# Ropes moved inside a branch, indexer heads in pairs, samples' values in two passes, a final tile in halves: one change to a two-layer hybrid encoder

## The reference, cut to what matters

```
# mixer A: rotary on queries, keys and indexer; 4 indexer heads score all keys
a_q = rope(heads(a_q), pos);  i_q = rope(i_q.reshape(B, T, N_IDX, IDX_DIM), pos)
dots  = einsum('bqhd,bkd->bqhk', qi, ki) * IDX_DIM ** -0.5
score = einsum('bqhk,bqh->bqk', relu(dots), wi)
top_val, top_idx = top_k(where(adm, score, NEG), topk)      # then softmax over the chosen keys
# mixers B and C: v = xn @ w_v for 8 heads of 64, and attention over all admissible keys
branch = einsum('btnw,nwd->btnd', o, w_branch)
x = x + einsum('btnd,btnd->btd', sigmoid(xn @ w_gate), branch) @ w_out
x = x + (silu(g) * u) @ w_down                              # g, u: convolved rows of rmsnorm(x) @ w_up
y = rmsnorm(x, norm_final)
```

## Time and profile before

| | |
|---|---|
| median of 3 executions | 2195.29 us (2191.95 to 2202.59) |
| profiled execution, its own time | 2195.33 us |
| its span | 2193.5 us |
| TensorE (PE) busy | 2148.7 us, 98% |
| VectorE (DVE) busy | 1342.6 us, 61% |
| ScalarE (ACT) busy | 955.0 us, 44% |
| mean granted TensorE clock | 0.995 of full speed |

### The profile page before, as it was taken

The page is one execution under the profiler, slowest core; times in us unless marked ns, Lnnn a source line. Parts: engine busy times, 40 slices in busy tenths (PEclk is TensorE's granted clock), DMA queues, the critical chain, the costliest instruction groups (busy, mean ns, idle before and its releaser), DMA issues.

```text
span 2193.5 us, 40057 instructions
## 1 busy us (share of the span) xinstructions
PE 2148.7 (98%) x16226; PEld 2023.5 (92%) x16226; DVE 1342.6 (61%) x2486; ACT 955.0 (44%) x1543; POOL 196.0 (9%) x144
## 2 busy tenths in 40 slices
PE   7999999999999999999999999999999999999997
PEld 7798999897899999999998889888979999999997
DVE  6558636765566773576365686377656477636753
ACT  3346414634634662344332572156255266524432
POOL 0000000000022110011310100000000311100122
PEclk9999999999999999999999999999999999999998
DMA  5231133121122223222232212221211222232223
GB/s 193 59 108 40 58 97 111 40 78 39 49 78 77 86 86 87 87 85 87 96 104 68 92 39 87 84 95 49 71 40 55 84 80 80 88 91 86 86 87 103
DMA packets 51795, 176.10 MB, mean 80 GB/s; under 512 B 6032, under 2 KB 8672, under 8 KB 51664
## 3 DMA queue, kind: packets, MB, share of 16 engines
q1 hardware_dynamic: 44496, 158.81, 23.4%
q0 software_dynamic: 2848, 10.54, 1.2%
q10 hardware_dynamic: 4320, 4.87, 0.7%
HBM read 161.30 MB, written 12.90 MB: 79 GB/s over the span
## 4 chain that ended last, share of the span: by engine, by line
PE 96%; DVE 3%; ACT 1%; DMA 0%; issue 0%; SPq 0%; DVEq 0%; ACTq 0%
PE d L1230 61%; PE d L1273 14%; PE ab L1306 4%; PE ab L1527 2%; PE d L1570 2%; PE d L1579 2%; PE d L1306 1%; PE d L1444 1%; PE ab L1352 1%; PE ab L1230 1%; PE ab L1557 1%; PE ab L1519 1%; PE ab L1520 1%; DVE ol L813 1%; PE ab L1257 0%; PE d L1398 0%
## 5 line engine op out<-in xcount | busy, mean ns | idle before, releaser
L410 ACT ACTIVATE wh<-raw 128x512 fp32r<-128x512 f32 x580 | 365.7, 631 | 839.6 <-PE d L1230 697.0
L710 DVE TENSOR_TENSOR wl<-raw,wh 128x512 fp32r<-128x512 f32 x580 | 402.8, 696 | 410.0 <-ACT wh L410 400.6
L1230 PE MATMUL d<-xh,wh 128*128 128x288 f32 x2400 | 513.9, 295 | 17.7 <-DMA cf<-in_const 14.5
L1230 PE MATMUL d<-xl,wh 128*128 128x288 f32 x2400 | 510.4, 293 | 0.0
L1230 PE MATMUL d<-xh,wl 128*128 128x288 f32 x2400 | 510.4, 293 | 0.0
L1230 PEld LDWEIGHTS d<-xh,wh 128*128 128x128 f32 x2400 | 383.1, 188 | 21.2 <-DMA cf<-in_const 14.5
L1230 PEld LDWEIGHTS d<-xh,wl 128*128 128x128 f32 x2400 | 382.6, 188 | 0.0
L1230 PEld LDWEIGHTS d<-xl,wh 128*128 128x128 f32 x2400 | 382.4, 188 | 0.0
L1273 PE MATMUL d<-xh,wh 128*128 128x288 f32 x768 | 174.8, 309 | 0.0
L1273 PE MATMUL d<-xh,wl 128*128 128x288 f32 x768 | 164.9, 296 | 0.0
L1273 PE MATMUL d<-xl,wh 128*128 128x288 f32 x768 | 164.8, 296 | 0.0
(11 more groups left out here) (309 smaller groups left out, 3197.9 us busy)
## 6 DMA issues: line engine op xcount, KB each, us to landing
raw<-in_w SPq DMA_DIRECT2D x290, 512.0 KB, 3.5
out_o_k<-k POOLq DMA_DIRECT2D x4, 1152.0 KB, 7.2
out_o_v<-v POOLq DMA_DIRECT2D x4, 1024.0 KB, 8.7
x<-in_xT SPq DMA_DIRECT2D x8, 288.0 KB, 6.4
out_y<-z SPq DMA_DIRECT2D x8, 288.0 KB, 2.3
k<-in_bc_k_past ACTq DMA_DIRECT2D x4, 512.0 KB, 4.7
v<-in_bc_v_past ACTq DMA_DIRECT2D x4, 512.0 KB, 5.6
cf<-in_const SPq DMA_DIRECT2D x1, 896.0 KB, 8.1
```

The lines of the kernel that those rows point to most:

```text
L410: act.activation(wh[:, c % SPLIT_SLOTS, :], raw[v_ % 2][:, (c % 2) * 512:(c % 2) * 512 + 512], ACT.Copy).then_inc(high_done, 1)
L710: dve.tensor_tensor(wl[:, c % SPLIT_SLOTS, :], raw[(c // 2) % 2][:, (c % 2) * 512:(c % 2) * 512 + 512], wh[:, c % SPLIT_SLOTS, :].bitcast( ...
L1230: ins = pe.matmul(outs[half], w_, r_[:, kk, HALF * half:HALF * half + HALF], start=first and n == 0, stop=last and n == len(kks) - 1)
```

## The change

What it does, part by part:

1. **Start.** `cf` is loaded after the second raw unit, masks after the third; TensorE waits for `s_const` only before the first `norm_sum`, which now stands in the middle of the third projection. ACT and DVE split six chunks in the opening instead of four. The casts of the constants move behind the first takes on DVE (`constants()`).
2. **Indexer.** Heads 0 and 1, then 2 and 3, go together: one head in rows 0 to 63 of the array, the other in rows 64 to 127, in two banks. Steps stand between half projections (`project_half`). The sums of the forget gate on DVE move into the projection of values.
3. **Values.** For the samples `xp` holds the 64 high columns and the 64 low columns of x side by side (`pair_samples`, two DVE copies per branch). The fifth token tile then takes 2 passes, not 3; DVE adds the two row halves.
4. **B, p = 0.** Four gate blocks stand ahead of `logits_x`.
5. **A.** `turn_query(2)` and `turn_query(3)`, with their ropes, move into pairs 0 and 1, behind the second `turn`; `scores_next(0)` waits for the second rope only and stands between the halves of query projection 3. DVE and ACT order follows.
6. **Branch output.** `branch_first` does the high products of j = 0 and j = 1, then the low products of both.
7. **FFN norm.** The square of the last tile of x is made by ACT and added by DVE; Pool squares seven tiles.
8. **End.** The last tile is computed for tokens 0 to 287, then 288 to 575, each with its own norm and outputs; 16 stores. The two weight units beyond the end are not loaded any more.

The core of the diff:

```diff
@@ sync @@
+            sp.dma_start(raw[1][:], w[1]).then_inc(landed[1], 16)
             sp.dma_start(cf[:], const).then_inc(s_const, 16)
-            sp.dma_start(raw[1][:], w[1]).then_inc(landed[1], 16)
-            sp.dma_start(w1[:, 0:M_END], masks).then_inc(s_masks, 16)
...
@@ vector @@
                 low_parts(l, 9)
+                if l == 0:
+                    constants()
+                pair_samples()
                 wait_taken(dve, l, D_KI)
                 rope(l, 0, ki, norm_both)
...
+            def pair_samples():
+                dve.tensor_copy(xp[:, :, 0:TS], xh[:, :, TP:T].bitcast(F32))
+                dve.tensor_copy(xp[:, :, TS:2 * TS], xl[:, :, TP:T].bitcast(F32)).then_inc(samples_paired, 1)
...
                 for m in (B, C, A):
                     for j in range(2 if m == B else 0, 4):
+                        if m == B:
+                            index_adds(j - 2, 0)
+                            index_adds(j - 2, 1)
+                        if m == A and j == 3:
+                            scale_step(l, m, 0, 0)
                         low_parts(l, 2 * U_Q[m] + 2 * j + 4)
...
-                        if m == A and j:
+                        if m == A and j in (1, 2):
                             wait_taken(dve, l, D_Q[m] + j - 1)
                             rope(l, 2 + j, q[:, j - 1, :], perm_both)
...
                         gate_take(l, m, 2 * p)
+                        if m == A and p < 2:
+                            rope(l, 5 + p, q[:, 2 + p, :], perm_both)
                         max_step(l, m, p, 3)
...
+                dve.wait_ge(acc_ready, 2 * l + 2)
+                dve.wait_ge(last_square, l + 1)
+                dve.tensor_tensor(sumsq[:], sumsq[:], tmp[:], ALU.add).then_inc(last_sum, 1)
@@ gpsimd @@
-                for j in range(KD):
+                for j in range(KD - 1):
                     wait_taken(pool, l, D_OUT + j)
                     square(j)
@@ tensor @@
             def branch_first(l, m):
...
                 pe.wait_ge(dfree[d % 2], freed(l, d))
+                for j in range(2):
+                    pe.wait_ge(low_done, l * CHUNKS + c + j + 1)
+                    for kk in range(4):
+                        if j == 0:
+                            pe.wait_ge(oh_ready, l * 12 + 4 * m + kk + 1)
+                        products(j, kk, wh, oh, first=kk == 0)
+                        products(j, kk, wl, oh)
+                    if j == 0:
+                        pe.wait_ge(o_ready, l * 3 * PAIRS + PAIRS * m + PAIRS)
+                        pe.sem_inc(dfree[1 - gate_bank(m)], HEADS)
+                        pe.wait_ge(dfree[(d + 1) % 2], freed(l, d + 1))
+                for j in range(2):
+                    for kk in range(4):
+                        if j == 0:
+                            pe.wait_ge(ol_ready, l * 12 + 4 * m + kk + 1)
+                        ins = products(j, kk, wh, ol, last=kk == 3)
+                    ins.then_inc(chunks, 1)
...
+                for w_, f_, l_ in ((wh, True, False), (wl, False, True)):
+                    ins = pe.matmul(src(4), xp[:, kk, :], w_[:, c % SPLIT_SLOTS, cols:cols + n],
...
-            pe.wait_ge(s_const, 16)
...
+                def index_heads(pair, s):
+                    if pair or s > 1:
+                        pe.wait_ge(relus, l * 8 + 4 * pair + s - 1)
+                    if s < 3:
+                        t = I_QT[s]
+                        for i, r in enumerate(ROWS):
+                            ins = pe.matmul(ab[:, 2 * (s % 2) + i, 0:tile_keys(t)], iq[r, pair, t * P:(t + 1) * P], k2[r, 1, 0:tile_keys(t)], start=True, stop=True)
+                    else:
+                        for a, n, key in ((0, PAST, T), (PAST, TS, TP)):
+                            for r in ROWS:
+                                ins = pe.matmul(ab[r, 2, a:a + n], iq[r, pair, TP:T], k2[r, 1, key:key + n], start=True, stop=True)
...
+                        for pair in range(2):
+                            index_heads(pair, 0)
+                            index_heads(pair, 1)
+                            project_half(l, U_Q[B] + 2 + pair, D_Q[B] + 2 + pair, 0)
+                            index_heads(pair, 2)
+                            index_heads(pair, 3)
+                            project_half(l, U_Q[B] + 2 + pair, D_Q[B] + 2 + pair, 1)
...
-                            project(l, U_Q[A] + 3, D_Q[A] + 3)
-                            turn_query(2)
-                            gate_blocks(l, m, 0, range(0, 2))
-                            turn_query(3)
-                            gate_blocks(l, m, 0, range(2, 4))
-                            pe.wait_ge(roped, l * 8 + 8)
+                            project_half(l, U_Q[A] + 3, D_Q[A] + 3, 0)
+                            pe.wait_ge(roped, l * 8 + 6)
                             scores_next(0)
+                            project_half(l, U_Q[A] + 3, D_Q[A] + 3, 1)
+                            gate_blocks(l, m, 0, range(0, 4))
...
+                            if m == A and p < 2:
+                                turn_query(2 + p)
+                                gate_blocks(l, m, 2 * p + 1, range(0, 2))
+                                pe.wait_ge(roped, l * 8 + 7 + p)
+                                scores_samples(p)
+                                gate_blocks(l, m, 2 * p + 1, range(2, 4))
...
+            down_half(0, range(FH)).then_inc(first_half, 1)
+            down_half(1, range(0, 4))
+            pe.wait_ge(acc_ready, 1 + 2 * LAYERS)
+            sum_half(0, sumsq, stop=False)
+            pe.wait_ge(last_sum, LAYERS + 1)
+            sum_half(0, tmp, start=False).then_inc(norms, 1)
+            sum_half(1, sumsq, stop=False)
+            down_half(1, range(4, FH)).then_inc(chunks, 3)
+            pe.wait_ge(last_sum, LAYERS + 2)
+            sum_half(1, tmp, start=False).then_inc(norms, 1)
```

More of the change, by code:

```diff
@@ L680, in _ @@
                     round_a(f, FH - 1)
-                    for c in range(24):
+                    last = f and l == LAYERS - 1
+                    if last:
+                        act.preload_act_table_set("natural_log_exp_and_others")
+                    for c in range(24 - SPLIT_SLOTS if last else 24):
                         high_part(l * CHUNKS + f * (2 * U_HALF), l * (UNITS // 2) + f * (U_HALF // 2), 2 * U_DOWN + 4 + c)
@@ L1230, in dense @@
                             ins = pe.matmul(outs[half], w_, r_[:, kk, HALF * half:HALF * half + HALF],
-                                            start=first and n == 0, stop=last and n == len(kks) - 1)
+                                            start=first and n == 0 and begin, stop=last and n == len(kks) - 1 and end)
                     if n % 4 == 3 or n == len(kks) - 1:
@@ L1236, in no_wait, with sum_half @@
                 pass
+            def sum_half(half, squares, start=True, stop=True):
+                return pe.matmul(norm_out[half], cf[:, C_ONE:C_ONE + P], squares[:, HALF * half:HALF * half + HALF], start=start, stop=stop)
             def norm_sum(count):
-                pe.wait_ge(acc_ready, count)
-                for half in range(2):
-                    ins = pe.matmul(norm_out[half], cf[:, C_ONE:C_ONE + P], sumsq[:, HALF * half:HALF * half + HALF], start=True, stop=True)
-                ins.then_inc(norms, 1)
+                if count % 2:
+                    pe.wait_ge(acc_ready, count)
+                else:
+                    pe.wait_ge(last_sum, count // 2)
+                sum_half(0, sumsq)
+                sum_half(1, sumsq).then_inc(norms, 1)
             def xn_wait(l, r):
@@ L1290, in branch_first, with products @@
-                pe.wait_ge(o_ready, l * 3 * PAIRS + PAIRS * m + PAIRS)
-                pe.sem_inc(dfree[1 - gate_bank(m)], HEADS)
-                for kk in range(4):
-                    pe.wait_ge(ol_ready, l * 12 + 4 * m + kk + 1)
-                    for half in range(2):
-                        ins = pe.matmul(dhalf[d % 2][half], hi_w[:, kk * P:kk * P + P], ol[:, kk, HALF * half:HALF * half + HALF],
-                                        start=False, stop=kk == 3)
-                ins.then_inc(chunks, 1)
+                def products(j, kk, weights, heads, first=False, last=False):
+                    for half in range(2):
+                        ins = pe.matmul(dhalf[(d + j) % 2][half], weights[:, (c + j) % SPLIT_SLOTS, kk * P:kk * P + P],
+                                        heads[:, kk, HALF * half:HALF * half + HALF], start=first, stop=last)
+                    return ins
@@ L1304, in by_token @@
                     o = src(t)
                     for x_, w_, f_, l_ in ((xh, wh, True, False), (xh, wl, False, False), (xl, wh, False, True)):
-                        ins = pe.matmul(o, x_[:, kk, a:a + P], w_[:, c % SPLIT_SLOTS, cols:cols + n],
-                                        start=first and f_ and starts(t), stop=last and l_, skip_group_check=True)
```

(10 more changed lines are left out.)

350 lines of the change are left out of this document (205 added, 145 removed).

## The result

The changed kernel took 2180.28 us (four executions, 2179.25 to 2181.17), the kernel before 2195.36 us in the same comparison. The ratio is 0.993, 95% interval 0.990 to 0.995: faster, by 15 us and not by the 42 forecast, and outside the range of 2145 to 2165. The profiled execution has a span of 2177.4 us.

What follows compares the result with a forecast made beforehand. PE, busy 98% of the span, was taken as the bound, leaving only matmul time and its pauses or slow stretches. Eight terms, -5.0 -10.6 -7.4 -2.6 -12.0 +3.0 -3.0 -4.5 = -42.1, took 2195.3 to 2153 us; range 2145 to 2165.

Steps and rivals of the forecast that it cites:

- At the upper level a 288-column matmul costs 0.13 us: All TensorE work at the 2.4 GHz granted clock: one price per matmul, 6.4 us for a projection of 48.
- the first rival: Branch A: new waits eat more, each bringing some 3 us at 1.2 GHz; +12, 2165 us; 0.22 together with head-pair rival.
- a sign of being wrong: Anywhere in the kernel: a PE wait over 3 us or a mean clock under 0.99 would disprove the forecast.
- The spell at the lower level: Branch A, kernel before: some 3 us per layer lost to the lower clock after PE's waits.
- its list of signs: Whole kernel: expected trace marks, such as first matmul near 8.3 us and 10.4 us from last matmul to end.
- the second (no overlap of heads): Indexer: head pairs don't overlap; +9.6 us, 2163 us; chance 0.22 together with the first rival.
- the third (hidden waits): Rope waits (4.8 us) or bank waits (7.8 us) are hidden after all: 2148 or 2145, both 2140; chance 0.14.
- the fourth (a lower clock: TensorE throughout: fewer pauses lower the granted clock; 21.5 us per hundredth, about 2205 us at 0.97; chance 0.02.
- the fifth: Somewhere in the new order: an unseen wait keeps the change from doing what it says; 2170 to 2190 us; chance 0.05.

Runs made afterwards that it cites:

- e13: Changed kernel with the FFN's norm sum issued two matmuls later in both layers, no instruction added; 2159.21 us.
- e3: Changed kernel with the FFN norm change alone undone, so Pool squares the last x tile again; 2163.78 us.
- e15: Changed kernel with the FFN's norm sum issued four matmuls later in the first layer, six in the second; 2170.06 us.
- e11: Changed kernel with DVE making the constants and sample pairs later, in idle time; 2175.59 and 2176.19, 2166.34 and 2166.50 us.
- e5: Changed kernel with the branch output change alone undone, going tile by tile again; 2155.20 us.
- e4: Kernel before with the FFN norm change alone: ACT squares the last x tile, DVE adds it; 2191.03 us.
- e6: Changed kernel with extra 288-column matmuls right ahead of the FFN's norm sum, two in the first layer, four in the second; 2170.97 us.
- e1: Changed kernel with two extra 512-column matmuls right behind each layer's norm sum in the FFN; 2180.67 us.
- e2: Changed kernel with extra 512-column matmuls in varied numbers behind FFN norm sums, in branch outputs and ahead of second projections; 2176.69 us.
- e10: Changed kernel with A's output tile by tile, earlier B/C takes, later constants, plus 512-column probes in five branch outputs and an extra matmul before layer 1's norm sum; 2160.60 us.

## Why the prediction was wrong, step by step

The step that failed is not one of the eight parts: it is the sentence "At the upper level a 288-column matmul costs 0.13 us", used as if the more than 10,000 of them that the change leaves alone would keep their price: a term of zero, without a reason given. The runs showed +21.0 us in its place, at 133.3 instead of 130.0 ns a matmul. The rivals had a price for the clock, but the clock was 0.998; what changed was the rhythm at the same clock. Whether the rows of the kernel before could have shown it is another matter: its stretch behind branch A already ran at 133.3 ns (592 successive distances in layer 1), and I took one price for all. With the norm sum moved by two matmuls, the changed kernel takes 2159.2, inside the range; 6 us are then left against 2153, half of them in part 1. Another 1.7 or so is a spell that the first rival had in mind, only elsewhere: in the profile of e13, and in those of e3 and e15, the wait of 3.4 us for the small tile is followed by 3.4 us of matmuls 0.24 apart. The changed kernel's own profile has none there (start:end, length, PE busy, granted clock, DMA share, GB/s; e13 first):

```profile
42.90:46.90 4.00, 4.00 (x21) 0.57 0.46 135
```

```profile
42.70:46.70 4.00, 3.98 (x31) 1.00 0.47 135
```

From the starts of like instructions in the two traces, the profiled 16.1 us come together so (us, to 0.2):

| stretch | forecast | measured |
|---|---|---|
| start to the first query projection (part 1) | -5.0 | -1.9 |
| layer 1: B (parts 2, 3, 4, 6) | -8.35 | -8.4 |
| layer 1: C (parts 3, 6) | -1.75 | -1.7 |
| layer 1: A to the norm sum (parts 5, 6, 7) | -6.2 | -6.3 |
| FFN of layer 1 | 0 | +10.7 |
| layer 2: B, C | -10.1 | -9.9 |
| layer 2: A to the norm sum | -6.2 | -4.9 |
| FFN of layer 2 | 0 | +10.2 |
| end (part 8) | -4.5 | -4.0 |

**Part 1** was mis-sized. The second projection ended at 23.47 instead of 22.2 (28.53 before): PE needed 48 matmuls from 8.14 to 17.07, 22 of them 0.24 or more apart, at the lower level; the matmuls began 6.4 us earlier than before, but the clock rose only 4.0 us earlier. The wait behind the small tile was 3.4 instead of 1.3, over the 3 us that the prediction itself had named as a sign of being wrong: before it DVE runs without a gap from 33.89, and I had put its spare time at 1.1 us. With the casts gone from there it still was 1.2 (e11), so the spare time was nearer to nothing.

**Part 2** right: 3.02 us a pair, forecast 3.2; the samples of two heads, which write one bank, 0.69, forecast 0.7, where one head alone took 2.81 - 2.20 = 0.61. By the rule of the Trainium skill, TensorEngine Tiling (Array Packing), "Gotcha 1: PSUM Pressure", the two heads could not have overlapped and would have taken twice 0.61; the measurement bears out. **Part 3** right: 3.26. **Part 4** right: the wait is gone, and none came for `hx`. **Part 5** right in layer 1; each rope cost 0.95 (a distance of 1.08 for 0.13), forecast 1.2. In layer 2 it brought 1.3 us less, because the kernel before had less to lose there. The spell at the lower level that the prediction put at some 3 us per layer was shorter in its layer 2. From the end of C's output to the start of A's, layers 1 and 2, before (first two lines) and after:

```profile
475.67:606.34 130.67, 126.25 (x1027) 0.97 0.17 50
1557.50:1686.73 129.23, 124.81 (x1028) 0.99 0.16 50
```

```profile
463.74:588.38 124.64, 122.42 (x1024) 1.00 0.17 52
1540.07:1664.70 124.63, 122.41 (x1024) 1.00 0.17 52
```

**Part 6** right in its direct price (a wait of 1.1 and a distance of 1.41 for 0.13, so 1.28 against 1.3, in all six) and wrong in what hung on it: its stall in branch A is where the cycle began whose wrong place the norm sum met. Undoing it alone brought 25 us (e5), eight times the 3.0 of the sum. **Part 7** right: each `xl` ahead of an FFN's norm sum took 0.81 to 0.82; alone it brought 4.3 (e4), forecast 3.0, bound 3.4. It had a second effect that no row of mine could show: it took away the stall that used to set the place behind branch A's. **Part 8** right, half a microsecond short: 9.5 us from the last matmul's taker and 1.46 for the sums ahead of the last matmuls make 11.0, where 10.4 was the forecast for both together (its list of signs has the 10.4 from the last matmul on, which leaves the sums out).

Of the rivals the first (1.2 GHz spells in A: the granted clock there is 1.00) and the second (no overlap of heads) did not occur, nor the third (hidden waits), nor the fourth (a lower clock; by its own 21.5 us a hundredth, a mean of 0.97 gives 2207 and not 2205). The time lies within the fifth's 2170 to 2190, but by luck: its mechanism was a wait, and there was none. The clock was not under 0.99; the one sign of being wrong that did come, the wait over 3 us, cost 3 us and not 27.

## What to carry to other kernels

Where a kernel is one long stream of equal matmuls, compare the mean distance of starts in the untouched stretches before and after, not only waits and clock: a rise of 2.5% in it was worth half of a well-counted gain of 42 us. A time forecast should then hold a term for it, one price per long stretch. If executions of one kernel fall into groups a fixed step apart, look for a long stretch whose length differs by that step between the groups. And where a pair of odd instructions can be moved by two places at no cost, such a rhythm is cheap to win: here 21 us. The place has then to be read from the trace, and not from the time alone: in e6 and e15 the time fitted the forecast with the layers exchanged.

## What the runs showed of the hardware

At the same granted clock (1.00) a stream of 288-column float32r matmuls, each with its own weight load, has two lasting rates, 130.0 and 133.3 ns. Which one follows a norm sum (fp32, distances 242) goes by its place in the long rhythm's cycle of four matmuls, and moving it by two, without any other instruction, turned some 6270 matmuls (2180.3 to 2159.2 us), and in the other direction too (2195 to 2214). Why the cycle exists stays open, and so does why the 512-column matmuls of the value projections are followed by the short rate each time, while extra ones (e1, e2, e10) were only once.

What sets the cycle's beginning at a stall stays open too, but its length goes with it. Ten traces hold 55 stalls on the bank of the third tile, all with a distance between 1402 and 1406 ns. After 1405 or 1406 ns the first 140 came at the 6th or 14th distance (32 of 32), after 1402 or 1403 at the 12th or 16th, which is two places on in a cycle of four (7 of 7); after 1404 at the 14th (14) or the 12th (2). So stalls that differ by a few nanoseconds go with different places, and a place with 10.7 us. No run set this length as a test.

The Trainium skill, TensorE: Matmul & The Clock Gate, "Back-to-back issue gap", gives columns / 2.4 + 2.5 ns as the distance of isolated matmuls at the upper clock, an estimate of 122.5 ns for 288 columns. It says that in a stream of weight loads and matmuls both set the spacing, and has no figure for 288 columns there. Both rates of this case lie above that estimate, by 7.5 and 10.8 ns, and a single figure can't tell them apart; the measurement decides. Which of the two instructions makes the cycle no run here shows.
